# Feed-forward layers cut into three stretches of feature tiles instead of two, with one output weight piece per output tile

## The reference

```python
D_FF = 2816
def swiglu(x, w_in, w_out):
    gate, up = jnp.split(x @ w_in, 2, axis=-1)
    return (jax.nn.silu(gate) * up) @ w_out

def macaron_layer(x, mixer, ...):
    x = x + FFN_HALF * rmsnorm(swiglu(rmsnorm(x, ffn1_pre_g), ffn1_w_in, ffn1_w_out), ffn1_post_g)
    x = x + rmsnorm(mixer(rmsnorm(x, mix_pre_g)), mix_post_g)
    x = x + FFN_HALF * rmsnorm(swiglu(rmsnorm(x, ffn2_pre_g), ffn2_w_in, ffn2_w_out), ffn2_post_g)
    return x
```

## Time and profile before

| what | value |
|---|---|
| median of 3 runs (lowest, highest) | 3333.84 us (3322.33, 3336.97) |
| the profiled execution's span | 3333.7 us |
| PE busy, matmuls | 3161.7 us (95%), x17800 |
| DVE busy | 1652.0 us (50%) |
| ACT busy | 1199.2 us (36%) |
| POOL busy | 685.7 us (21%) |
| input pieces of the feed-forward parts | x176, 512.0 KB, 3.4 us to landing |
| output pieces of the feed-forward parts | x128, 384.0 KB, 3.0 us to landing |

### The profile page before, as it was taken

One profiled execution on the slowest core, in us unless ns is written; L12 is line 12 of the kernel. 1 busy time (PEld: TensorE's weight loads), 2 busy tenths in 40 slices (PEclk: granted clock), 3 DMA queues, 4 the chain that ended last, 5 costly groups with the idle time before them and its releaser, 6 DMA issues.

```text
span 3333.7 us, 43230 instructions
## 1 busy us (share of the span) xinstructions
PE 3161.7 (95%) x17800; PEld 2514.6 (75%) x17800; DVE 1652.0 (50%) x2636; ACT 1199.2 (36%) x2094; POOL 685.7 (21%) x579
## 2 busy tenths in 40 slices
PE   6999999899999999999789999999999999999998
PEld 3877677677777788877677788888888885588886
DVE  2155564436674534475654553446444525564344
ACT  3242264443263322342343432234222415542222
POOL 3234314334514000045221200000000243220000
PEclk8999999999999999999677999999999999999999
DMA  6213211221102332232000233232232230022322
GB/s 230 95 36 133 95 31 40 70 73 52 60 13 80 105 99 94 91 101 81 8 8 2 70 100 109 92 109 78 90 107 86 86 108 32 2 98 89 110 83 82
DMA packets 78740, 260.50 MB, mean 78 GB/s; under 512 B 8528, under 2 KB 11728, under 8 KB 77392
## 3 DMA queue, kind: packets, MB, share of 16 engines
q1 hardware_dynamic: 77680, 253.02, 23.5%
q0 software_dynamic: 864, 4.72, 0.4%
HBM read 255.61 MB, written 2.10 MB: 77 GB/s over the span
## 4 chain that ended last, share of the span: by engine, by line
PE 83%; DVE 8%; ACT 4%; POOL 2%; issue 1%; DMA 1%; SPq 0%; ACTq 0%; DVEq 0%; POOLq 0%
PE banks L363 81%; PE banks L372 2%; POOL w_lo L354 1%; DVE x_lat L708 1%; DVE w_lo L354 1%; DVE area L705 1%; DMA area<-in_w_mod 1%; ACT w_hi L344 0%; DVE small L2080 0%; POOL area L428 0%; DVE area L2029 0%; DVE area L636 0%; DMA w_raw<-in_l_ffn_w_in 0%; DVE area L546 0%; DVE w_late L354 0%
## 5 line engine op out<-in xcount | busy, mean ns | idle before, releaser
L363 PE MATMUL banks<-area,w_hi 128*128 128x512 f32 (+4 forms) x5980 | 1745.4, 375 | 28.6 <-POOL w_lo L354 13.0
L363 PEld LDWEIGHTS banks<-area,w_hi 128*128 128x128 f32 (+2 forms) x5980 | 1084.3, 188 | 277.8 <-issue 31.8
L363 PE MATMUL banks<-area,w_lo 128*128 128x512 f32 (+4 forms) x2990 | 1108.5, 372 | 0.0
L363 PEld LDWEIGHTS banks<-area,w_lo 128*128 128x128 f32 (+2 forms) x2990 | 561.9, 188 | 110.6
L363 PE MATMUL banks<-area,w_late 128*128 128x512 f32 (+2 forms) x2370 | 554.0, 384 | 8.1 <-DVE w_late L354 5.3
L344 ACT ACTIVATE w_hi<-w_raw 128x1024 fp32r<-128x1024 f32 (+2 forms) x353 | 341.3, 970 | 540.9 <-PE banks L363 405.6
L363 PEld LDWEIGHTS banks<-area,w_late 128*128 128x128 f32 (+1 forms) x2370 | 429.8, 188 | 108.4 <-DVE w_late L354 6.6
L363 PE MATMUL banks<-area,area 64*64 64x32 f32 (+11 forms) x4424 | 402.8, 316 | 64.9 <-DMA area<-in_w_mod 15.7
L363 PEld LDWEIGHTS banks<-area,area 64*64 64x64 f32 (+4 forms) x4424 | 309.0, 175 | 146.9 <-issue 59.8
L428 POOL TENSOR_TENSOR area<-area,area 128x512 f32<-128x512 f32 (+1 forms) x72 | 92.6, 1290 | 1379.3 <-ACT area L413 1377.8
L354 POOL TENSOR_TENSOR w_lo<-w_raw,w_hi 128x1024 fp32r<-128x1024 f32 (+1 forms) x124 | 284.8, 2299 | 403.5 <-ACT w_hi L344 403.4
(11 more groups left out here) (259 smaller groups left out, 2474.9 us busy)
## 6 DMA issues: line engine op xcount, KB each, us to landing
w_raw<-in_l_ffn_w_in SPq DMA_DIRECT2D x176, 512.0 KB, 3.4
w_raw<-in_l_ffn_w_out SPq DMA_DIRECT2D x128, 384.0 KB, 3.0
w_raw<-in_w_in SPq DMA_DIRECT2D x66, 512.0 KB, 3.5
w_raw<-in_w_mod SPq DMA_DIRECT2D x32, 512.0 KB, 4.4
w_raw<-in_w_qkv SPq DMA_DIRECT2D x24, 512.0 KB, 3.5
w_raw<-in_l_w_in SPq DMA_DIRECT2D x22, 512.0 KB, 3.5
w_raw<-in_w_out SPq DMA_DIRECT2D x32, 320.0 KB, 2.9
area<-in_w_mod SPq DMA_DIRECT2D x8, 1024.0 KB, 16.6
```

The source lines that it names most:

```text
L363: return e.matmul(out, lhsT, rhs, start=first, stop=stop, skip_group_check=True)
```

## The change

A table of three stretches, tiles 0 to 7, 8 to 15 and 16 to 21, takes the place of the two halves of 11. A stretch has as many feature tiles as one output piece can hold, so every output tile has one output piece per stretch: 8 feature tiles (128x1024) in the first two, 6 (128x768) in the third. The second and the third stretch add to y, and the third is the final one, with the squares and the two token halves at its end. The buffers of the products shrink from 11 tiles to 8.

```diff
-FFN_K = (6, 5)
+FFN_PHASES = ((0, 8), (8, 16), (16, 22))
...
-            for half in range(2):
-                for c in range(FT):
-                    yield (name + "_w_in", half * FT + c, True)
-                for c in range(16):
-                    yield (name + f"_w_out{half}", c, True)
+            for p, (j0, j1) in enumerate(FFN_PHASES):
+                for c in range(2 * j0, 2 * j1):
+                    yield (name + "_w_in", c, True)
+                for c in range(8):
+                    yield (name + f"_w_out{p}", c, True)
...
-        APART_AT = work_at + 4 * (2 * (FT // 2) + 4) * T
+        APART_AT = work_at + 4 * 26 * T
...
-                self.a_hi, self.a_lo = place.take(n_half, T, dtype=f32r), place.take(n_half, T, dtype=f32r)
+                self.a_hi, self.a_lo = place.take(8, T, dtype=f32r), place.take(8, T, dtype=f32r)
...
+                for p, (j0, j1) in enumerate(FFN_PHASES):
+                    project = Project([(name + "_w_in", c) for c in range(2 * j0, 2 * j1)], P, self.norm, T)
                     out = ProjectOut(
-                        name, lambda m, half=half: [(name + f"_w_out{half}", 2 * m, FFN_K[0]),
-                                                    (name + f"_w_out{half}", 2 * m + 1, FFN_K[1])],
-                        [(self.a_hi[:, k, :], self.a_lo[:, k, :]) for k in range(n_half)], T, y_sb, self.add.squares,
-                        lambda q, k, half=half: q.wait_ge(*at(name, "a", half, k)), add=(half == 1), final=(half == 1))
+                        name, lambda m, p=p, n=j1 - j0: [(name + f"_w_out{p}", m, n)],
+                        [(self.a_hi[:, k, :], self.a_lo[:, k, :]) for k in range(j1 - j0)], T, y_sb, self.add.squares,
+                        lambda q, k, p=p: q.wait_ge(*at(name, "a", p, k)), add=p > 0, final=p == len(FFN_PHASES) - 1)
...
-                            if half and j == 0:
-                                q.wait_ge(*at(*self.halves[0][1].finished()))
+                            if p and j == 0:
+                                q.wait_ge(*at(*self.parts[p - 1][1].finished()))
...
-                    if half:
+                    if out.final:
                         e.preload_act_table_set("natural_log_exp_and_others")
...
-        w = I[n + "_w_out_2"].reshape(2, FT // 2, P, D)
-        for half in range(2):
-            arr[n + f"_w_out{half}"] = by_k_runs(w[half], FFN_K[:2])
+        w = I[n + "_w_out_2"].reshape(FT, P, D)
+        for p, (j0, j1) in enumerate(FFN_PHASES):
+            arr[n + f"_w_out{p}"] = by_k_runs(w[j0:j1], (j1 - j0,))
```

More of the change, by code:

```diff
@@ L1188, in __init__ @@
                 self.add = HalfAdd(name, lambda j, s: half_g[:, f, j:j + 1], y_sb, Area(post_at))
-                self.halves = []
-                for half in range(2):
-                    project = Project([(name + "_w_in", half * FT + c) for c in range(FT)], P, self.norm, T)
+                self.parts = []
+                for p, (j0, j1) in enumerate(FFN_PHASES):
+                    project = Project([(name + "_w_in", c) for c in range(2 * j0, 2 * j1)], P, self.norm, T)
                     out = ProjectOut(
-                        name, lambda m, half=half: [(name + f"_w_out{half}", 2 * m, FFN_K[0]),
-                                                    (name + f"_w_out{half}", 2 * m + 1, FFN_K[1])],
-                        [(self.a_hi[:, k, :], self.a_lo[:, k, :]) for k in range(n_half)], T, y_sb, self.add.squares,
-                        lambda q, k, half=half: q.wait_ge(*at(name, "a", half, k)), add=(half == 1), final=(half == 1))
-                    self.halves.append((project, out))
-                self.first = self.halves[0][0].pieces[0]
+                        name, lambda m, p=p, n=j1 - j0: [(name + f"_w_out{p}", m, n)],
+                        [(self.a_hi[:, k, :], self.a_lo[:, k, :]) for k in range(j1 - j0)], T, y_sb, self.add.squares,
+                        lambda q, k, p=p: q.wait_ge(*at(name, "a", p, k)), add=p > 0, final=p == len(FFN_PHASES) - 1)
+                    self.parts.append((project, out))
+                self.first = self.parts[0][0].pieces[0]
             def x_event(self, s, j):
@@ L1203, in lead_dve @@
             def lead_dve(self, q, e):
-                for m, s, c0, c1, u, bank in itertools.islice(self.halves[0][0].each(), self.LEAD):
+                for m, s, c0, c1, u, bank in itertools.islice(self.parts[0][0].each(), self.LEAD):
                     q.wait_ge(*at("projected", u))
@@ L1209, in pe @@
             def pe(self, q, e):
-                for half, (project, out) in enumerate(self.halves):
-                    project.pe(q, e, lead=0 if half else self.LEAD)
+                for p, (project, out) in enumerate(self.parts):
+                    project.pe(q, e, lead=0 if p else self.LEAD)
                     out.pe(q, e)
             def act(self, q, e):
-                for half, (project, out) in enumerate(self.halves):
+                for p, (project, out) in enumerate(self.parts):
                     for m, s, c0, c1, u, bank in project.each():
@@ L1237, in dve @@
                         sg, a = self.sg[j % 2], self.a[j % 2]
-                        lead = not half and m < self.LEAD
+                        lead = not p and m < self.LEAD
                         q.wait_ge(*at("evicted" if lead else "projected", u))
```

25 lines of the change are left out of this document (12 added, 13 removed).

## The result

| | us, median (lowest to highest), runs | ratio to before, 95% interval |
|---|---|---|
| before, beside the changed kernel | 3333.76 (3322.33 to 3338.41), 13 | |
| changed | 3342.32 (3337.65 to 3346.53), 13 | 1.0028 [1.0019, 1.0038] |

In microseconds the ratio is 9.3 [6.3, 12.7]; the two medians differ by 8.6. The profiled execution took 3344.02 us, with a span of 3342.3. So the change costs a little and brings nothing, at 3342 against a forecast of 3343.

What follows compares the result with a forecast made beforehand. PE, 83% of the chain, was taken as the bound, so the change acts only where PE waits, at the parts' ends. 2.4 + 1.25 + 2.4 + 1.75 = 7.8, plus 1.5 for clock, 9.3 us: 3343 us, range 3334 to 3352.

Steps and rivals of the forecast that it cites:

- Inside a part, nothing: Within each feed-forward part: extra additions and fewer output pieces lie beside 320 us of unbroken matmuls, so both count zero.
- The rival of a tile too short for its queue: Third stretch: if an output tile needs 4.8 us, eight tiles lose 0.6 each, 3361 us in total; chance 0.05.
- Zero 3.5 us later: End of a part: the moment when DVE can add output tile 6 (zero) comes 3.5 us later than before.
- The mixer borders, h0 at +4.95: Two mixer borders: the last tile's first half (h0) is added 4.95 us after zero; each border costs 2.4 us.
- Piece 4's split out of the border: Stage borders: the split of the next stage's weight piece 4 leaves the border's chain, gaining 1.15 us each.
- The border behind `l0_ffn2`: At that border DVE also splits pieces 0 and 1; h0 is added at +4.25, costing 1.25 us.
- The end of the program: End of `l1_ffn2`: h0 is added at +2.1, the same chain follows, and the program ends 1.75 us later.
- The clock: Stage borders: PE idling brings one half-clock loss of 1.5 us for the three borders, with bounds 0 and 4.5.
- cheap ends: Ends of parts: splits and POOL's additions miss each other, the clock stays up; cost 5.0 us, 3339 us; chance 0.20.
- nothing at the border: Borders: PE's own work bounds them, the later start costs nothing, only gains of 3 x 1.15 stand; 3330 us; chance 0.07.
- a clock that falls at every border: All three borders: half clock at each, 7.8 + 3 x 2.5 = 15.3 us, 3349 us; chance 0.10.
- PE's wait that I ascribed to h0's square: Mixer borders: PE should wait 2 to 3 us on ACT for the square of h0.

Runs made afterwards that it cites:

- The stretch of six first: Changed kernel with stretches of 6, 8 and 8 feature tiles instead of 8, 8 and 6: 3334.19 us, ratio 1.0005.
- splits on DVE: Changed kernel with the mixers' weight pieces 0 and 1 split by DVE instead of POOL: 3343.38 us, ratio 1.0033.
- h0 first: Changed kernel with the last output tile's first half (h0) added and squared ahead of the next stage's weight piece 4: 3337.48 us, ratio 1.0017.
- piece 4 in the border: Changed kernel with the next stage's weight piece 4 dealt with in the border again, not ahead of h0's addition: 3344.53 us, ratio 1.0040.
- two output pieces: Changed kernel with two output pieces per output tile in each stretch instead of one: 3365.6 us, ratio 1.0109.

## Why the prediction was right

*Inside a part, nothing.* Right: pieces of 1368 matmuls at 0.2335 us, no wait at a stretch's start, and no wait for weights in the third stretch. The rival of a tile too short for its queue fell. One reading was slightly off: the first output matmul starts at 1188.01 and DVE reads the bank behind it at 1188.21, 0.20 us later and not 0.27, so that the room of a stretch of six is 0.42 us and not 0.35.

*Zero 3.5 us later.* Right to the hundredth, 339.44 against 335.94 us behind the factor.

*The mixer borders, h0 at +4.95.* Measured +5.10 and +5.17, with the steps in the forecast's order: the additions of squares behind POOL's splits, tile 5's square waiting for POOL, piece 3's split held up by an addition. Tile 6 is added at +1.40, where I had 1.3. Net of the clock, the two borders cost 2.55 and 2.6 us, not 2.4. The stretch of six first gives the term from its other side: without the short last tile it vanishes.

*Piece 4's split out of the border.* Right: from L705 to the next factor it is 33.48 us instead of 34.62, 1.14 less, behind `l0_ffn2`. With the piece put back it was 34.62 again at the second mixer border, which has no half clock.

*The border behind `l0_ffn2`.* h0 at +4.28 (predicted +4.25), the interval 1.28 us longer (predicted 1.25).

*The end of the program.* h0 at +2.10, and the same chain behind it. Without its half clock, the interval is 1.6 us longer; predicted were 1.75.

*The clock* was mis-sized. I took one half clock of 1.5 us for the three borders; there were two, one that cost 1.5 us and one only about 0.5, in a stretch in which PE waited anyway (from h0's addition to the next factor 37.64 and 36.61 us, against 36.09 in the kernel with splits on DVE, whose mixer borders have none). That is 2.0 instead of 1.5, within the bounds. It is luck in part, since the three other kernels that end in a short stretch and leave pieces 0 and 1 to POOL had 2, 3 and 2. The forecast did not count the half clocks at the starts of the parts, which come in both kernels. The changed kernel's profile has two more of those than that of before, 3.1 us of its span. That half clocks make up much of the few microseconds by which runs of one kernel differ is likely from the times of the first factor above, and not shown.

The local terms add up to 2.55 + 1.28 + 2.6 + 1.6 = 8.0 and 2.0 for the clock, 10.0 us, against 7.8 + 1.5 in the forecast and 9.3 [6.3, 12.7] measured. The two profiled spans differ by 8.6 us: these 10.0, 3.1 for the half clocks at the starts, and 4.6 the other way outside the parts. The last two vary from one execution to the next, so the closeness of the total is partly luck; what was right are the terms in the parts. *The rivals:* cheap ends (5.0 us) fell with h0 at +5.1 and the border's half clocks; nothing at the border fell with the intervals; a clock that falls at every border fell, since one of three had none.

*What the forecast did not carry far enough* showed in the experiments. PE's wait that I ascribed to h0's square (2 to 3 us) is in truth two, 1.03 us on POOL and 1.16 on the square. Taking only the second away leaves the first, and behind it PE's own arrival at the sum, which is why h0 first and piece 4 in the border each gained 0.7 us per border less than expected of them.

## What to carry to other kernels

Here the cut of a reduction into stretches moved nothing inside, but its last stretch set how much matrix work lay beside the chain that ends the stage: where there must be a short stretch, don't put it last. By itself no cut into three beat the two halves (1.0005 and 1.0006 at best). When weight pieces grow to fill a buffer, count what stands ahead of the last addition in each engine's list, and of every wait that you remove, ask which engine is the next one late. And look at the waits that all versions share: one call moved ahead of a factor gave more than any order of stretches.

## What the runs showed of the hardware

*A short idle can halve the clock.* Behind the wait for piece 6, the granted clock was 0.50 (1.2 GHz) for 3.41 us in 20 of the 36 parts of nine profiles, at 7.8 to 8.9 us behind the factor, and 1.00 (2.4 GHz) throughout in the other 16, with the same rows in front. It costs 1.53 us (321.01 against 319.48). Where the wait was taken away it came in none of eight parts. That the wait is its cause is shown by this.

What decides between the two outcomes can be read from the same traces. In each of them, the starts of all records at 0.50 lie on one even grid, to 0.02 us, whatever the kernel does in between. In the 20 parts with a half clock the wait begins 0.11 to 1.13 us behind a point of that grid; in none of the other 16 does it. The grid lies differently against the start of the program in each of the eleven profiles, so that the outcome looks like chance to whoever reads one of them. The Trainium skill (TensorE: Matmul & The Clock Gate, "What's actually happening") says that the monitor which sets the clock runs free of the program, so that the same kernel meets it in another phase each time. The traces agree, with one profile of each kernel here.

*Half clocks in the borders.* They came in 9 of 12 borders of the four kernels which end in a short stretch and have POOL split pieces 0 and 1, and in none of 21 borders of the other seven. In 18 of these 21 no wait of PE reaches 1 us. In the three others, where DVE splits, PE waits 0.2 to 0.3, 1.16 and 1.48 us, and that they have no half clock does not show that the place of the splits keeps it away: the same wait of 1.48 us goes both ways. It occurs in 11 borders. It began 0.05 to 0.59 us behind a point of the grid in five, all with a half clock, two of them behind `l0_ffn2` with only 0.24 us of wait on POOL before it (piece 4 in the border, and h0 first). It began 1.21 us or more behind one in six, among them the three with splits on DVE, and all six are without. Of the other four half clocks, three stand by waits of 4.35 to 5.04 us (two output pieces), and one behind 1.11 and 1.16 us in close succession (changed kernel, second mixer border).

*DVE and POOL shut each other out.* A full split takes 1.22 us alone and 2.25 where it starts while POOL's additions run (1427.60, POOL until 1428.77), and moving POOL's splits away brought it to 1.48, with 0.4 us of an addition left to wait for. That agrees with the rule of the Trainium skill (SBUF — State Buffer, "Who interferes with whom") that the prediction cites.

*A wait is more than its idle time.* The wait of 1.78 us cost 2.04 us per part. Across it, two matmuls start 2.17 us apart (1090.31 and 1092.48) instead of 0.23, which is 1.94, and the next start comes 0.1 us later than usual. The idle is counted from the end of the last matmul's record, which is longer (0.39 us) than the distance between two starts.
